# Softmax blocks turned on VectorE in couples, and all sums of weights on VectorE

## The reference, cut to what matters

```
h = rms_norm(x, pre_norm); proj = h @ w_in
q, k, v, gate_a, u_b, v_b, gate_b, mg_a, mg_b = split(proj)
scores = where(in_window, q k^T / 8 + bias, -inf)      # 16 heads, 8 blocks of 128 queries, 256 keys
m = max(max(scores), sink); p = exp(scores - m)
probs = p / (sum(p) + exp(sink - m)); o_a = probs @ v
y_a = (o_a * silu(gate_a)) @ w_branch_a
o_b = gelu(u_b) * (tril(W_s) LN(gelu(v_b)) + b); y_b = (o_b * silu(gate_b)) @ w_branch_b
out = (sigmoid(mg_a) * y_a + sigmoid(mg_b) * y_b) @ w_out; x = x + rms_norm(out, post_norm)
```

## Time and profile before

| | |
|---|---|
| median of 3 runs | 901.44 us (901.38 to 901.56) |
| profiled execution | 901.18 us, its span 899.4 us |
| granted TensorE clock | 0.999 of full speed |
| TensorE | 892.2 us busy, 99% |
| VectorE | 632.3 us, 70% |
| GpSimd | 523.5 us, 58% |
| ScalarE | 502.0 us, 56% |

### The profile page before, as it was taken

One profiled execution on the slowest core, in us unless ns is written; L12 is line 12 of the kernel. 1 busy time (PEld: TensorE's weight loads), 2 busy tenths in 40 slices (PEclk: granted clock), 3 DMA queues, 4 the chain that ended last, 5 costly groups with the idle time before them and its releaser, 6 DMA issues.

```text
span 899.4 us, 12763 instructions
## 1 busy us (share of the span) xinstructions
PE 892.2 (99%) x4268; PEld 747.6 (83%) x4268; DVE 632.3 (70%) x1135; ACT 502.0 (56%) x982; POOL 523.5 (58%) x427
## 2 busy tenths in 40 slices
PE   9999999999999999999999999999999999999997
PEld 7888888888888888888888888888888888888886
DVE  6766795555555555546455589688789878989968
ACT  6554354776767676766766674344344434534562
POOL 4564335788888888887979667344442252042236
PEclk9999999999999999999999999999999999999999
DMA  9786664443434346534343453544188550435004
GB/s 316 189 198 150 223 208 106 153 108 104 135 103 131 106 126 159 174 107 132 103 136 93 121 156 106 188 150 122 43 321 300 188 210 1 141 128 200 1 1 187
DMA packets 170512, 130.90 MB, mean 146 GB/s; under 512 B 58552, under 2 KB 139472, under 8 KB 170320
## 3 DMA queue, kind: packets, MB, share of 16 engines
q1 hardware_dynamic: 168208, 126.66, 46.3%
q10 hardware_dynamic: 2240, 3.43, 1.1%
HBM read 93.87 MB, written 39.35 MB: 148 GB/s over the span
## 4 chain that ended last, share of the span: by engine, by line
PE 98%; DVE 1%; issue 0%; ACT 0%; DVEq 0%; POOLq 0%; POOL 0%; ACTq 0%
PE acc L1023 50%; PE acc L1205 11%; PE acc L876 10%; PE ps_m L1205 7%; PE ps_t L1205 7%; PE ps_t L1040 3%; PE ps_m L1071 3%; PE acc L966 2%; PE ps_t L1050 1%; PE ps_t L906 1%; PE ps_m L906 1%; PE ps_t L908 0%; PE acc L1097 0%; PE ps_m L908 0%; PE ps_t L892 0%
## 5 line engine op out<-in xcount | busy, mean ns | idle before, releaser
L1023 PE MATMUL acc<-mv,w_hi 128*128 128x512 f32 x1344 | 349.3, 391 | 0.0
L1023 PEld LDWEIGHTS acc<-mv,w_hi 128*128 128x128 f32 x1344 | 246.1, 188 | 46.5
L1023 PE MATMUL acc<-mv,w_lo 128*128 128x512 f32 x672 | 181.0, 391 | 0.0
L1820 POOL TENSOR_TENSOR w_lo<-sums,w_hi 128x1024 fp32r<-128x1024 f32 x48 | 117.7, 2454 | 62.2 <-ACT w_hi L1371 49.1
L1023 PEld LDWEIGHTS acc<-mv,w_lo 128*128 128x128 f32 x672 | 126.1, 188 | 28.0
L1820 POOL TENSOR_TENSOR w_lo<-raw,w_hi 128x1024 fp32r<-128x1024 f32 (+1 forms) x48 | 94.3, 1965 | 41.4 <-ACT w_hi L1364 34.3
L1575 ACT ACTIVATE prob<-neg_s,neg_max 128x129 f32<-128x129 f32 x128 | 50.7, 397 | 88.0 <-DVE neg_max L2152 87.9
L1205 PE MATMUL acc<-right,left 128*128 128x512 f32 x432 | 98.6, 389 | 0.0
L1205 PEld LDWEIGHTS acc<-right,left 128*128 128x128 f32 x432 | 81.0, 188 | 17.2 <-DVE left L2213 0.3
L876 PE MATMUL acc<-mv 128*128 128x512 f32 x288 | 69.4, 394 | 0.0
L1205 PE MATMUL ps_t<-right,left 128*128 128x512 f32 x288 | 67.2, 389 | 0.0
(11 more groups left out here) (286 smaller groups left out, 1702.1 us busy)
## 6 DMA issues: line engine op xcount, KB each, us to landing
raw<-in_w_in SPq DMA_DIRECT2D x56, 512.0 KB, 4.8
ht_d<-sums SPq DMA_DIRECT2D x8, 512.0 KB, 4.7
mix_d<-mix_b SPq DMA_DIRECT2D x8, 512.0 KB, 3.8
prob_d<-prob SPq DMA_DIRECT2D x32, 128.0 KB, 2.2
turned_in<-prob_d SPq DMA_DIRECT2D x128, 32.0 KB, 2.3
ga_d<-gate SPq DMA_DIRECT2D x16, 256.0 KB, 4.4
tb<-tb_d SPq DMA_DIRECT2D x4, 1024.0 KB, 5.3
ub<-mix_d SPq DMA_DIRECT2D x7, 512.0 KB, 3.5
```

The lines of the kernel that those rows point to most:

```text
L1023: ins = nc.tensor.matmul(bank, (w_lo if y == 2 else w_hi)[:, left + k * P:left + (k + 1) * P], right[:, (OPW if y == 1 else 0) + k * HALF: ...
L1820: nc.gpsimd.tensor_tensor(w_lo[:, c], src, w_hi[:, c].bitcast(f32), ALU.subtract).then_inc(wlo_ok, 1)
```

## The change

Every softmax block is now transposed by VectorE, in couples. Four stores of a couple, one for each 32 rows, put the 32x32 squares of four 128x128 matrices in their places in DRAM, in runs of 128 bytes, and one load brings the couple back as 128x512. TensorE's transposes and VectorE's cast and subtraction behind them are gone; the bank that they used is now a second one for the scores, which wait for the block before last. High part, low part and selection are made once for a couple: 512, 512 and 1024 columns. The order of steps moves: store at 3c + 3, load at 3c + 4, high part at 3c + 7, low part and selection at 3c + 8, both values at 3c + 9, o_tmp at 3c + 10, gate product at 3c + 11, for couple c = 0 to 3. The gate's first half has one buffer instead of two, and waits for the store of the head pair before. left_sums of pairs 1 to 16 move from GpSimd (steps 2 and 3) to VectorE: left_sums_1 in step 2 and left_sums_2 in step 3 of each pair, ahead of q_lo, gate_mul and c_22.

```
--- before.py
+++ after.py
@@ constants and buffers
-LAST_STEP = 20
+LAST_STEP = 22
+SOFT_W = 4 * P + 2
-        ps_s, ps_p = ps_t[:, 0:512], ps_t[:, 512:768]
+        ps_s = (ps_t[:, 0:512], ps_t[:, 512:1024])
+        def gate_w(p, h):
+            return gate[:, 0:HALF] if h == 0 else gate[:, (p % 2 + 1) * HALF:(p % 2 + 2) * HALF]
+        def couple_at(k, lag):
+            return [j for j in range(4) if 3 * j + lag == k]
@@ sync
             def prob_away(j):
-                sp.wait_ge(turn_ok, j + 1)
-                sp.dma_start(prob_d[j, :, :].rearrange("p (c j) -> p c j", c=2),
-                             prob[j % 2][:, :].rearrange("p (c j) -> p c j", c=2)[:, :, 0:P]).then_inc(prob_out, 16)
+                sp.wait_ge(turn_ok, 2 * j + 2)
+                for q in range(4):
+                    sp.dma_start(prob_d[j, :, :, :].rearrange("c (g a) (q b) -> q a c g b", g=4, q=4)[q],
+                                 prob[j % 2][32 * q:32 * (q + 1), 1:1 + 4 * P].rearrange("a (c g b) -> a c g b", c=4, g=4)
+                                 ).then_inc(prob_out[j % 2], 16)
             def prob_back(j):
-                sp.wait_ge(prob_out, 16 * (j + 1))
+                sp.wait_ge(prob_out[j % 2], 64 * (j // 2 + 1))
                 if j:
                     sp.wait_ge(pool_own, POOL_FRONT + j)
-                for g in range(4):
-                    sp.dma_start(turned_in[32 * g:32 * (g + 1), :].rearrange("a (c q b) -> a c q b", c=2, q=4),
-                                 prob_d[j, :, :].rearrange("(q a) (c g b) -> g a c q b", q=4, c=2, g=4)[g]).then_inc(prob_in, 16)
+                sp.dma_start(turned_in.rearrange("p (c x) -> p c x", c=4), prob_d[j, :, :, :].rearrange("c p x -> p c x")).then_inc(prob_in, 16)
-                for blk in even_at(k, 2):
-                    prob_away(4 * p + blk // 2)
-                for blk in even_at(k, 3):
-                    prob_back(4 * p + blk // 2)
+                for c in couple_at(k, 3):
+                    prob_away(4 * p + c)
+                for c in couple_at(k, 4):
+                    prob_back(4 * p + c)
-                if k in (13, 19):
+                if k in (15, 21):
@@ tensor
-                if s:
-                    pe.wait_ge(scores_used, s)
+                if s > 1:
+                    pe.wait_ge(scores_used, s - 1)
-            def transpose_p(p, blk):
...
-                for blk in odd_at(k, 6) + even_at(k, 7):
-                    values(p, blk)
-                for blk in odd_at(k, 3):
-                    transpose_p(p, blk)
+                for c in couple_at(k, 9):
+                    values(p, 2 * c)
+                    values(p, 2 * c + 1)
@@ scalar
-                nc.scalar.activation(pt_pack[0][:, 0:256], turned_in[:, :], ACT.Copy).then_inc(turn_hi, 1)
+                nc.scalar.activation(pt_pack[:, 0:512], turned_in, ACT.Copy).then_inc(turn_hi, 1)
-                for blk in even_at(k, 5):
-                    turned_hi(p, blk)
-                if k in (8, 11, 14, 17):
-                    g = (k - 8) // 3
+                for c in couple_at(k, 7):
+                    turned_hi(4 * p + c)
+                for g in couple_at(k, 10):
@@ gpsimd
-                for blk in even_at(k, 6) + odd_at(k, 3):
...
+                for c in couple_at(k, 8):
+                    j = 4 * p + c
+                    pool.wait_ge(turn_hi, j + 1)
+                    nc.gpsimd.tensor_tensor(pt_pack[:, 512:1024], turned_in, pt_pack[:, 0:512].bitcast(f32),
                                             ALU.subtract).then_inc(pool_own, 1)
...
+                        out=pt_prev[:, :].rearrange("p (y q) -> p y q", y=8),
+                        in_=pt_pack[:, :].rearrange("p (y q) -> p y q", y=8), compare_op=ALU.is_ge, fill=0.0,
+                        base=-1, pattern=[[0, 8], [-1, P]], channel_multiplier=1).then_inc(pt_ok, 1)
-                if k in (9, 12, 15, 18):
-                    g = (k - 9) // 3
+                for g in couple_at(k, 11):
             def after(n, s):
-                if s == 2 and n < FIRST_U:
-                    left_sums_1(n + 1)
-                    if n < FIRST_U:
-                        left_sums_2(n + 1)
@@ vector
+                if h == 0 and p >= 1:
+                    dve.wait_ge(ga_out[0], 16 * p)
+                if h == 1 and p >= 2:
+                    dve.wait_ge(ga_out[1], 16 * (p - 1))
-                for blk in odd_at(k, 3):
-                    s = 8 * p + blk
-                    dve.wait_ge(pt_done, s // 2 + 1)
...
-                    own.link(nc.vector.tensor_copy(pack[:, 0:256], ps_p))
-                    nc.vector.tensor_tensor(pack[:, 256:512], ps_p, pack[:, 0:256].bitcast(f32), ALU.subtract).then_inc(ptl_ok, 1)
-                for blk in even_at(k, 1):
+                for blk in blocks_at(k, 1):
                     dve.wait_ge(prob_ok, 8 * p + blk + 1)
-                if k in (8, 11, 14, 17):
-                    g = (k - 8) // 3
+                for g in couple_at(k, 10):
+                if s == (2 if n >= FIRST_U else 3):
+                    left_sums_2(n + 1)
                 if s == 2:
-                    if n >= FIRST_U:
-                        left_sums_2(n + 1)
+                    if n < FIRST_U:
+                        left_sums_1(n + 1)
```

More of the change, by code:

```diff
@@ L215, in build @@
             with ExitStack() as s1:
[L216 to L219, removed]
+                soft = sb("soft", [P, 2 * SOFT_W + 4 * SINK_W + 768], f32, s1)
+                gate = sb("gate", [P, 3 * HALF], f32, s1)
                 v_st = sb("v_st", [P, 2 * NT * P], f32r, s1)
@@ L222, in build @@
                     v_tmp = sb("v_tmp", [P, 2 * NT * P], f32r, lands)
-                pt_pack = [sb(f"pt_pack{b}", [P, 512], f32r, s1) for b in range(2)]
-                pt_prev = [sb(f"pt_prev{b}", [P, 512], f32r, s1) for b in range(2)]
-                neg_s = sb("neg_s", [P, 4 * SINK_W], f32, s1)
+                pt_pack = sb("pt_pack", [P, 1024], f32r, s1)
+                pt_prev = sb("pt_prev", [P, 1024], f32r, s1)
                 bias_t = sb("bias_t", [P, 512], f32, s1)
@@ L376, in build, with prob_at, prob_w, exp_w @@
         S1h, S2h = slice(0, HALF), slice(HALF, 2 * HALF)
+        prob = (soft[:, 0:SOFT_W], soft[:, SOFT_W:2 * SOFT_W])
+        turned_in = soft[:, 2 * SOFT_W:2 * SOFT_W + 512]
+        o_tmp = soft[:, 2 * SOFT_W + 512:2 * SOFT_W + 768]
+        neg_s = soft[:, 2 * SOFT_W + 768:2 * SOFT_W + 768 + 4 * SINK_W]
+        v_part = (soft[:, 0:SEQ], soft[:, SEQ:2 * SEQ])
+        def gate_w(p, h):
+            return gate[:, 0:HALF] if h == 0 else gate[:, (p % 2 + 1) * HALF:(p % 2 + 2) * HALF]
         def head(blk, h):
             return slice(blk % 4 * 2 + h, blk % 4 * 2 + h + 1)
-        def prob_w(s, h, width):
-            buf = prob[2] if s % 2 else prob[s // 2 % 2]
-            return buf[:, h * SINK_W:h * SINK_W + width]
+        def prob_at(s, h):
+            return 1 + ((1, 2) if s % 2 == 0 else (0, 3))[h] * P
+        def prob_w(s, h):
+            c = prob_at(s, h)
+            return prob[s // 2 % 2][:, c:c + P]
+        def exp_w(s, h):
+            c = prob_at(s, h) - (h == 0)
+            return prob[s // 2 % 2][:, c:c + SINK_W]
         def neg_w(blk, h):
@@ L1066, in values @@
                 kbs = (0,) if blk == 0 else (0, 1)
+                heads = slice(0, 4, 3) if blk % 2 else slice(1, 3)
                 for kb in kbs:
@@ L1569, in exps @@
                     act.wait_ge(sink_ok, p + 1)
-                if s % 2 and s > 1:
-                    act.wait_ge(pt_done, s // 2)
                 if s % 2 == 0 and s >= 4:
-                    act.wait_ge(prob_out, 16 * (s // 2 - 1))
+                    act.wait_ge(prob_out[s // 2 % 2], 64 * (s // 4))
                 for h in range(2):
-                    ins = nc.scalar.activation(prob_w(s, h, SINK_W), neg_w(blk, h), ACT.Exp, scale=-1.0, bias=neg_max[:, head(blk, h)],
+                    ins = nc.scalar.activation(exp_w(s, h), neg_w(blk, h), ACT.Exp, scale=-1.0, bias=neg_max[:, head(blk, h)],
                                                accum_out=row_sum[:, head(blk, h)])
@@ L1893, in left_sums_2 @@
-            def left_sums_2(n):
-                r0 = first_raw(n)
-                pool.wait_ge(sum_ok, 4 * n + 1)
-                nc.gpsimd.tensor_tensor(sums[:, 0:512], sums[:, 1024:1536], r0[:, 0:HALF], ALU.subtract).then_inc(sum_ok, 1)
-                pool.wait_ge(sum_ok, 4 * n + 3)
-                nc.gpsimd.tensor_tensor(sums[:, 1536:2048], r0[:, HALF:1024], sums[:, 0:512], ALU.subtract).then_inc(sum_ok, 1)
+                    nc.gpsimd.tensor_tensor(part, o_tmp, part, ALU.mult).then_inc(og_ok, 1)
@@ L2147, in attend @@
                         dve.wait_ge(exp_ok, s - 1)
+                    bank = ps_s[s % 2]
                     if blk > 0:
-                        own.link(nc.vector.copy_predicated(blocks(ps_s)[:, :, 1, :], before_i, blocks(ps_s)[:, :, 0, :]))
```

(3 more changed lines are left out.)

107 lines of the change are left out of this document (33 added, 74 removed).

## The result

The changed kernel takes 936.35 us, median of 4 runs (934.64 to 937.15), beside 901.41 for the kernel before (901.34 to 901.56). The ratio is 1.0385 with a 95% interval of 1.0367 to 1.0403. I forecast 915 and a range of 894 to 930. The sign was right. The size was not: 35 us instead of 14, and the time lies outside the range.

The account below looks back on a forecast made before the run. TensorE's matmuls, 892.2 of 899.4 us, were taken as the bound. 901.2 less 7.0 for transposes plus 20.5 for waits (1.7 + 0.4 + 0.8 = 2.9 a period, seven periods) gave 914.7, forecast as 915; range 894 to 930.

Parts of the forecast that it names:

- TensorE's gain: In the stage of product pairs, 64 transposes go, 0.22 us a pair: 7.0 us less for TensorE.
- T(5): Start of step 5's product on TensorE in a 14-step period; a wait of 0.8 us for ScalarE's eviction was forecast.
- T(12): Start of step 12's product on TensorE in a 14-step period; a wait of 0.4 us for ScalarE's eviction was forecast.
- Chain A: From product 5's eviction in the odd half to couple 0's values: 14.9 us against TensorE's 13.2, wait 1.7.
- Chain C: From T(12) to the eviction due at T(5): on time by 0.1 us without port meetings, 0.8 late with one.
- I take one, 0.8 after the margin: In Chain C, one VectorE-GpSimd port meeting of 0.9 us was assumed; none to three would cost 0 to 2.6.
- Chain B: From couple 0's values to the eviction in the even half, due at T(12): 8.9 us against 8.5, wait 0.4.
- SyncE and the DMAs: In SyncE's queue, stores land in 3 us and raw loads 1 to 5 us ahead of readers; no cost.
- Rival 2: The VectorE-GpSimd port decides: three meetings a period, each a whole 1.29 us operation, none hidden; 935 us, chance 0.08.
- Rival 1: In the pair stage all is hidden and only the transposes' 7.0 us come back: 894.2 us, chance 0.16.

Follow-up runs that it names:

- e7: The changed kernel with the sums back on GpSimd in their old steps, the couples' load two steps later and everything behind it one step later: 897.49 us.
- e11: The kernel of e7 timed again in five rounds: 896.70 us.
- e6: The changed kernel with the sums of pairs 1 to 16 cut to 16 columns, all instructions and semaphores in place: 915.8 us.
- e4: The changed kernel with left_lo of product 5 on GpSimd one step later, behind the couple's subtraction and selection: 957.38 us.
- e5: The changed kernel with the four stores of a couple in runs of 512 bytes, squares not placed: 930.62 us.
- e1: The changed kernel with the sums of pairs 1 to 16 back on GpSimd in their old steps, couples kept: 926.06 us.
- e3: The kernel before with the sums of pairs 1 to 16 on VectorE, left_sums_2 behind gate_mul and c_22: 915.95 us.
- e10: The kernel of e7 with the load of couple c back in step 3c + 4 instead of 3c + 6: 908.22 us.
- e8: The kernel of e7 with the sums on VectorE, left_sums_2 behind gate_mul and c_22: 916.52 us.

## Why the prediction was right in sign and wrong in size

- **TensorE's gain: right, a little small.** 7.0 forecast, or 0.88 a period. A period went from 46.7 to 45.6 us where nothing is late, 8.7 in eight. e7 and e11, with nearly nothing late, came to 897.5 and 896.7.
- **The places: right.** The waits are at T(5), in step 9 and at T(12), and for those releasers.
- **Chain A: right.** 1.7 forecast, 1.9 measured; its 14.9 us is 15.2, in e6 too. I had named left_lo(5) as the lever. The turned copy is done at 340.67, but left_lo(5) runs from 338.87 to 341.28, and the subtraction starts behind it at 341.23. The lever is small: e4 takes left_lo(5) away, and couple 0 still waits 1.44.
- **Chain C: right mechanism, term too small.** The step that failed is "I take one, 0.8 after the margin". The port is met three times. I had looked at the gate just ahead of T(5), which met a difference in all eight periods before (1592 to 1606 ns). After, that one is free, 0.68, and the gate of the other half meets left_lo(5) instead, 1.65 at 315.18. left_sums_2 meets the selection and the gate product, 1.46 and 1.11 instead of twice 0.69. Together 0.97 + 0.77 + 0.42 = 2.2 us in a period, and T(5) with the two steps ahead of it is late by 2.2 in four of seven periods (by 0.7 to 1.1 in the second, fifth and sixth). I had three meetings at 2.6 as the upper end, so the row was inside my bounds and my choice from them was wrong.
- **Chain B: term too small.** The step that failed is the sum that ends in "Wait 0.4": 0.8 at T(12) and 0.1 behind it in a normal period, in all eight. Its 8.9 us is 9.3. The other steps of B I have not compared one by one, so which of them grew is open.
- **SyncE and the DMAs: wrong.** The step that failed is "the raw loads land 1 to 5 us ahead of their readers" with "so I cost it nothing". I priced the stores by a landing of 3 us (3.5 by the median) and left out two things: SyncE's own time to issue them, up to 2.9 us each, and that the queue stands until the last one of couple 0 has landed, after 7.1 to 9.5 us in seven periods. The trace of the kernel before had both: the same x_both loads that I took the landing from took 0.59 to 4.53 us each to issue, and the fourth load of the first even block landed after 7.4. 9.6 us came from there, 8.8 of it in two of eight periods, and a third of that as the clock at 0.50. With pieces of 512 bytes (e5) they are gone, and 5.7 us of time with them; the rest is lost at T(5) instead.
- Together: C 7.6 short, B 5.0, raw weights 9.6, A 1.3, step 0 of the fifth period 1.0, pairs of kind U 0.3, which makes 24.8. TensorE had 1.7 us less to issue than I forecast, and 1.1 of small delays of the kernel before are gone. That leaves 22.0. The profiled execution took 936.7 instead of 914.7.
- **Rival 2** (the port decides, 935) comes near the time by another way. It took three meetings a period at a whole 1.29 us each. The trace has the three meetings, but they cost 2.2 us together, and the time of 936 has 9.6 us of late weights in it, which it did not have. That the time fits is luck. e6 takes both the sums' length and their meetings away and brings back 20.5 us; how much of that is the port's alone, no run here shows. e4 shows what two more meetings cost: 3.1 us a period.
- **Rival 1** (all is hidden, 894.2) is wrong for this kernel and nearly right for e7. What chain A lacks is distance, and one step more of it is what e7 gives. The lever that rival 1 named, GpSimd free of left_lo(5), takes 0.45 us off the wait in e4; left_hi a step earlier was not run.

The gate shows the port most clearly. One shape has two durations in the changed kernel (ns min/median/max):

```profile
L2088 DVE SCALAR_TENSOR_TENSOR gate<-c x8: 684/1655/1686, 163.8 to 521.7; 128x512 f32<-128x512 f32 x8
L2088 DVE SCALAR_TENSOR_TENSOR gate<-ev x8: 683/684/685, 173.3 to 533.6; 128x512 f32<-128x512 f32 x8
```

Beside the gate at 315.18 GpSimd was in a difference (its timeline):

```profile
313.88 2.40 POOL L1816 TENSOR_TENSOR w_lo<-sums,w_hi 128x1024 fp32r<-128x1024 f32 x1
```

At 315.18, 1.10 of it was left, and 1.10 + 0.68 = 1.78, against 1.65 measured. The sums at 353.33 and 354.82 and the two of e4 fit in the same way: what was left of GpSimd's instruction plus the sum's own time, less 0.13 to 0.14. The Trainium skill, "SBUF — State Buffer", section "SBUF: two separate sides", states the rule for a VectorE operation with two SBUF inputs, as these are, against a GpSimd operation that reads SBUF: the one that starts first has the shared ports for its whole instruction, and the other is blocked until then. These rows agree with it. So a meeting costs the rest of the other's instruction, and not a whole one, as I had priced rival 2.

The Trainium skill, "DMA: Bandwidth & Descriptors", section "Specifications", wants at least 512 bytes a transfer for full rate and has a read-modify-write below that. The landings of 3.5 us against 2.2 for the same 64 KB agree with the first; whether a read-modify-write is the reason, no run here shows.

## What to carry to other kernels

Where engines run in order, a step's cost is not its busy time. Follow the loop through every engine once round, and compare its length with the distance in time that the schedule gives it: 1.9 us too long, seven times, is 13 us. When an operation is moved, list what stands behind it (e1, e3), and what will then run beside it on the engine that shares its port, its followers included (e4). Cost a DMA twice, once for its landing and once for the queue that issues it, and look who waits behind it on that queue. Take the landing at that place in the period and not the median: the last of couple 0's stores took 7.1 to 9.5 us where the median was 3.5.

## What the runs showed of the hardware

- A store of 64 KB in pieces of 128 bytes took its issuing queue 0.52 us by the median and up to 2.88; in pieces of 512 bytes 0.43 and 1.40.
- A meeting of a VectorE operation and a GpSimd one cost the second the rest of the first, less 0.13 to 0.14 us (five rows of the change and e4). It goes both ways: GpSimd's gate product of 128x256 took 1.17 us at 303.44 beside a sum of VectorE, and 0.73 at 313.02.
- Waits of TensorE of 1.8 (e10) to 4.0 us (the change) were in several places followed by 3.4 or 6.8 us at a granted clock of 0.50: twice in the pair stage of the change (waits of 3.1 and 4.0), in every period of e4 (3.5 to 4.0), and never there in e5 and e8, whose longest waits are 1.7 and 1.5. A wait of 2.0 in e1 left no such spell. Step 12 behind the wait of 4.0 in the change took 5.33 us instead of 3.79.
